# Experts' scatter in a mixture-of-experts kernel: the block outputs become the stationary operand, the residual reads the sums, the last round gathers nothing, and the output leaves in four parts

## What is computed

```
h2 = rms(x) * (1 + sc2) + sh2                       # 256 tokens x 1024
idx, w = the 8 best of 64 experts for each token    # weights sum to 2.5
moe  = (silu(h2 @ w_sh_gate) * (h2 @ w_sh_up)) @ w_sh_down                # shared expert
moe += sum over the token's experts e of
       w_e * ((silu(h2 @ w_gate_e) * (h2 @ w_up_e)) @ w_down_e)           # hidden width 256
out = x + gt2 * moe
```

## Time and profile before

| | |
|---|---|
| median of 3 runs | 1740.06 us (1738.6 to 1741.92) |
| profiled execution, its own time | 1738.21 us |
| its span, first to last instruction | 1736.6 us |
| mean granted clock | 0.986 |
| PE busy | 1661.4 us, 96% of the span |
| DVE, ACT busy | 971.8 us (56%), 688.5 us (40%) |
| pairs of blocks (count of L2944) | 34 |
| scatter matmuls, L1431 | 140 with `yhi`, 140 with `ylo`: 35 scatters of 8 |

### The profile page before, as it was taken

How to read it: one execution, slowest core, us unless ns; L and a number is a source line. 1 busy time by engine, 2 the same in 40 slices (tenths; PEclk the granted TensorE clock), 3 DMA queues, 4 the chain that set the end, 5 groups by cost and what they waited for, 6 DMA issues and landing times.

```text
span 1736.6 us, 26907 instructions
## 1 busy us (share of the span) xinstructions
PE 1661.4 (96%) x10642; PEld 1309.8 (75%) x10642; DVE 971.8 (56%) x1705; ACT 688.5 (40%) x1225; POOL 62.0 (4%) x48
## 2 busy tenths in 40 slices
PE   8889999998989999999999999999999999999997
PEld 6678999986789999878898989897544454545453
DVE  6967777769677777576756697665121212121212
ACT  2155434321554444465543577632222232323222
POOL 0100000001000000005110000000000000000000
PEclk9999999999999999999999999998999999999999
DMA  6222666752226667532402333336899999999993
GB/s 278 97 74 101 228 230 242 262 198 97 95 100 219 236 242 290 200 122 96 141 25 98 146 132 135 142 139 269 327 423 422 421 422 422 422 422 422 423 422 137
DMA packets 63963, 404.66 MB, mean 233 GB/s; under 512 B 12928, under 2 KB 14464, under 8 KB 15232
## 3 DMA queue, kind: packets, MB, share of 16 engines
q1 hardware_dynamic: 63440, 401.86, 59.3%
q10 hardware_dynamic: 432, 1.51, 0.2%
HBM read 401.91 MB, written 1.44 MB: 232 GB/s over the span
## 4 chain that ended last, share of the span: by engine, by line
PE 76%; DVE 16%; ACT 5%; issue 1%; DMA 0%; SPq 0%; DVEq 0%; ACTq 0%
PE ps L1441 20%; PE ps L847 19%; PE ps L988 10%; DVE big L2234 5%; PE ps L1414 4%; PE ps L1431 4%; PE ps L672 2%; DVE inv L2487 2%; DVE wlo L2298 2%; ACT whi L1634 2%; PE ps L1321 1%; DVE wlo L2665 1%; PE ps L1353 1%; PE ps L1382 1%; ACT wb L1842 1%
## 5 line engine op out<-in xcount | busy, mean ns | idle before, releaser
L2298 DVE TENSOR_TENSOR wlo<-ring,whi 128x2048 fp32r<-128x2048 f32 x76 | 174.2, 2292 | 90.3 <-ACT whi L1634 90.0
L847 PE MATMUL ps<-hg_hi,whi 128*128 128x272 f32 (+1 forms) x672 | 191.3, 285 | 2.4 <-DVE big L2430 2.4
L847 PE MATMUL ps<-hg_hi,wlo 128*128 128x272 f32 (+1 forms) x672 | 191.4, 285 | 0.0
L847 PE MATMUL ps<-hn_lo,whi 128*128 128x272 f32 (+1 forms) x672 | 190.8, 284 | 0.0
L1441 PE MATMUL ps<-big 128*64 128x512 f32 x816 | 181.8, 594 | 0.7 <-ACT big L2122 0.7
L1441 PE MATMUL ps<-ring,big 128*64 128x512 f32 x816 | 181.7, 594 | 0.0
L1634 ACT ACTIVATE whi<-ring 128x2048 fp32r<-128x2048 f32 x76 | 144.9, 1907 | 70.4 <-PE ps L847 51.8
L2951 DVE TENSOR_TENSOR ylo<-ps,yhi 128x512 fp32r<-128x512 f32 x68 | 47.0, 692 | 172.2 <-ACT yhi L2145 137.3
L672 PE MATMUL ps<-hn,ring 128*128 128x272 f32 x576 | 138.3, 398 | 0.0
L1441 PEld LDWEIGHTS ps<-big 128*64 128x64 f32 x816 | 57.5, 137 | 106.9 <-issue 106.6
L1441 PEld LDWEIGHTS ps<-ring,big 128*64 128x64 f32 x816 | 57.1, 137 | 107.2 <-issue 106.8
(11 more groups left out here) (456 smaller groups left out, 3585.9 us busy)
## 6 DMA issues: line engine op xcount, KB each, us to landing
ring<-in_stream SPq DMA_DIRECT2D x277, 1024.0 KB, 5.4
big<-in_stream SPq DMA_DIRECT2D x102, 1024.0 KB, 10.6
h<-in_xT SPq DMA_DIRECT2D x1, 1088.0 KB, 5.1
out_xT<-h SPq DMA_DIRECT2D x1, 1024.0 KB, 4.7
big<-in_consts ACTq DMA_DIRECT2D x1, 896.0 KB, 4.7
cst<-in_consts SPq DMA_DIRECT2D x1, 576.0 KB, 6.1
cs<-in_c_rows SPq DMA_DIRECT2D x1, 512.0 KB, 17.6
big<-in_consts ACTq DMA_DIRECT2D x1, 326.5 KB, 3.5
```

Source lines behind the costliest of these rows:

```text
L847: m = mm(out, a[:, at_:at_ + P], b[:, kept], start=first and i == 0, stop=last and i == 2)
L2298: v.tensor_tensor(wlo[j][:, :], ring[:, j, :], whi[d % 3][:, :], ALU.subtract).then_inc(wlo_ready, 1)
```

## The change

The scatter swaps its operands: 128 features of `yhi` or `ylo` are now stationary, and all 256 tokens of `STr` move. The sums then have features on the partitions, as `x` has them. `shared_down`, which starts these sums, is turned in the same way. The copies, the transposes back and their buffer and semaphores go, and DVE reads banks 4 to 7 itself. The fixed loop has 15 rounds (`FIXED`), the loop of `quads_n` follows, and the last round stands behind both as straight code without the next round's gather, its copies and its places. The last scatter is done in two halves, each after its own half of `ylo`. The output leaves in four transfers of two chunks each.

```diff
+FIXED = EXPERTS // 4 - 1
...
-            sp.wait_ge(x_ready, 24)
-            sp.dma_start(out, x).then_inc(out_done, 16)
-            sp.wait_ge(out_done, 16)
+            for i in range(4):
+                sp.wait_ge(x_ready, 16 + 2 * i + 2)
+                sp.dma_start(out[:, 2 * i:2 * i + 2, :], x[:, 2 * i:2 * i + 2, :]).then_inc(out_done, 16)
+            sp.wait_ge(out_done, 64)
...
+            def sums_of(c):
+
+                return ps[:, 4 + c // 2, (c % 2) * T:(c % 2 + 1) * T]
+
             def shared_down(t):
-                for half in range(2):
+                for c in range(4 * t, 4 * t + 4):
                     for f_ in range(2):
-                        m = mm(ps[:, 4 + 2 * t + half, :], hid[:, f_, t * P:(t + 1) * P], w_sh[:, f_, half * 512:(half + 1) * 512],
-                               start=f_ == 0, stop=False, skip_group_check=True)
+                        m = mm(sums_of(c), w_sh[:, f_, c * P:(c + 1) * P], hid[:, f_, :], start=f_ + c % 2 == 0, stop=False,
+                               skip_group_check=True)
                 return m
...
             def scatter(q, quarters=range(4), last=False):
 
-                for t, half in (divmod(quarter, 2) for quarter in quarters):
-                    for i, piece in enumerate((yhi, ylo)):
-                        m = mm(ps[:, 4 + 2 * t + half, :], STr[:, q, t * P:(t + 1) * P],
-                               piece[:, half * 512:(half + 1) * 512], start=False, stop=last and i == 1,
-                               skip_group_check=True)
+                for quarter in quarters:
+                    for c in range(2 * quarter, 2 * quarter + 2):
+                        for i, piece in enumerate((yhi, ylo)):
+                            m = mm(sums_of(c), piece[:, c * P:(c + 1) * P], STr[:, q, :], start=False, stop=last and i == 1,
+                                   skip_group_check=True)
                     if last:
                         m.then_inc(acc_full, 1)
...
-            def pair_of_blocks(quad, q, turn2):
+            def pair_of_blocks(quad, q, turn2, last=False):
...
-                if q == 1:
+                if q == 1 and not last:
                     pe.wait_ge(place_ready, 2 * quad + 4)
                     gather(0)
...
-                else:
+                elif not last:
                     gather(1)
...
-                turn_places(1 - q)
+                if q == 0 or not last:
+                    turn_places(1 - q)
...
-            with pe.Fori(0, EXPERTS // 4) as t_:
+            with pe.Fori(0, FIXED) as t_:
                 for q in range(2):
                     pair_of_blocks(t_, q, t_)
...
-                    pair_of_blocks(EXPERTS // 4 + t_, q, EXPERTS // 4 + t_)
-            pe.wait_ge(ylo_ready, EXPERTS + 4 * quads_n + 2)
-            scatter(1, last=True)
-
-            pe.wait_ge(acc_out, 4)
-            for k in range(DC):
-                for t in range(2):
-                    m = nc.tensor.transpose(ps[:, k // 2, (k % 2) * T + t * P:(k % 2) * T + (t + 1) * P],
-                                            acc_sb[:, t, k * P:(k + 1) * P], ident)
-                if k % 2:
-                    m.then_inc(y_full, 1)
+                    pair_of_blocks(FIXED + t_, q, FIXED + t_)
+            for q in range(2):
+                pair_of_blocks(FIXED + quads_n, q, FIXED + quads_n, last=True)
+            for half in range(2):
+                pe.wait_ge(ylo_ready, 4 * FIXED + 4 * quads_n + 5 + half)
+                scatter(1, range(2 * half, 2 * half + 2), last=True)
...
-            def pair_on_act(quad, q):
+            def pair_on_act(quad, q, last=False):
...
-                if q == 1:
+                if q == 1 and not last:
                     tokens_out(quad + 1, 0)
...
-                if q == 1:
+                if q == 1 and not last:
                     for i in range(1, 4):
                         tokens_out(quad + 1, i)
-                places_out(p + 1, 1 - q)
+                if q == 0 or not last:
+                    places_out(p + 1, 1 - q)
...
-            for g in range(2):
-                act.wait_ge(acc_full, g + 1)
-                f(acc_sb[:, 0, g * 512:(g + 1) * 512], ps[:, 4 + g, :], ACT.Copy).then_inc(acc_out, 1)
+            for q in range(2):
+                pair_on_act(FIXED + quads_n, q, last=True)
...
-            def pair_on_dve(quad, q):
+            def pair_on_dve(quad, q, last=False):
...
-                if q == 0:
+                if q == 0 and not last:
                     dve.wait_ge(t_full, p + 2)
                     places(quad + 1)
...
-            for g in range(2, 4):
-                dve.wait_ge(acc_full, g + 1)
-                v.tensor_copy(acc_sb[:, 1, (g - 2) * 512:(g - 1) * 512], ps[:, 4 + g, :]).then_inc(acc_out, 1)
+            for q in range(2):
+                pair_on_dve(FIXED + quads_n, q, last=True)
             for c in range(DC):
                 if c % 2 == 0:
-                    dve.wait_ge(y_full, c // 2 + 1)
-                v.scalar_tensor_tensor(x[:, c, :], flat[:, c * T:(c + 1) * T], mod[:, 40 + c:41 + c], x[:, c, :],
+                    dve.wait_ge(acc_full, c // 2 + 1)
+                v.scalar_tensor_tensor(x[:, c, :], flat[:, 2048 + c * T:2048 + (c + 1) * T], mod[:, 40 + c:41 + c], x[:, c, :],
                                        ALU.mult, ALU.add).then_inc(x_ready, 1)
```

More of the change, by code:

```diff
@@ L309, in build @@
         hg = region(27776, DC, 2 * P)
-        acc_sb = region(15488, 2, D)
         flat = ps[:, :, :].rearrange("p a b -> p (a b)")
@@ L469, in build @@
         acc_full = sem("acc_full")
-        acc_out = sem("acc_out")
-        y_full = sem("y_full")
         block = ctx.enter_context(nc.Block())
@@ L2151, in _ @@
             places_out(0, 0)
-            with act.Fori(0, EXPERTS // 4) as t:
+            with act.Fori(0, FIXED) as t:
                 for q in range(2):
@@ L2158, in _ @@
                 for q in range(2):
-                    pair_on_act(EXPERTS // 4 + t, q)
-            for g in range(2):
-                act.wait_ge(acc_full, g + 1)
-                f(acc_sb[:, 0, g * 512:(g + 1) * 512], ps[:, 4 + g, :], ACT.Copy).then_inc(acc_out, 1)
+                    pair_on_act(FIXED + t, q)
+            for q in range(2):
+                pair_on_act(FIXED + quads_n, q, last=True)
         @block.vector
@@ L2951, in pair_on_dve @@
                     v.tensor_tensor(ylo[:, o], ps[:, 3 - half, :], yhi[:, o], ALU.subtract).then_inc(ylo_ready, 1)
-            with dve.Fori(0, EXPERTS // 4) as t:
+            with dve.Fori(0, FIXED) as t:
                 for q in range(2):
@@ L2959, in _ @@
                 for q in range(2):
-                    pair_on_dve(EXPERTS // 4 + t, q)
-            for g in range(2, 4):
-                dve.wait_ge(acc_full, g + 1)
-                v.tensor_copy(acc_sb[:, 1, (g - 2) * 512:(g - 1) * 512], ps[:, 4 + g, :]).then_inc(acc_out, 1)
+                    pair_on_dve(FIXED + t, q)
+            for q in range(2):
+                pair_on_dve(FIXED + quads_n, q, last=True)
             for c in range(DC):
                 if c % 2 == 0:
-                    dve.wait_ge(y_full, c // 2 + 1)
-                v.scalar_tensor_tensor(x[:, c, :], flat[:, c * T:(c + 1) * T], mod[:, 40 + c:41 + c], x[:, c, :],
+                    dve.wait_ge(acc_full, c // 2 + 1)
+                v.scalar_tensor_tensor(x[:, c, :], flat[:, 2048 + c * T:2048 + (c + 1) * T], mod[:, 40 + c:41 + c], x[:, c, :],
                                        ALU.mult, ALU.add).then_inc(x_ready, 1)
```

## The result

| | before | after |
|---|---|---|
| median of 5 runs each | 1739.28 us (1738.55 to 1741.92) | 1730.51 us (1729.94 to 1732.69) |
| profiled execution, its span | 1736.6 us | 1730.9 us |
| first round's gate product to the end of the span | 515.75 us | 507.49 us |

The ratio is 0.9950, 95% interval 0.9936 to 0.9965: 8.8 us faster by the medians, with 9.0 forecast (1731.1 us, range 1728 to 1736). That the medians came within 0.2 us of the forecast is partly luck: further down, two medians of the same code lie 1.6 us apart, and the stretches add up to less than 9.0.

What follows compares the result with a forecast made beforehand. PE was taken to set the pace in the rounds, with transfers close behind, and a path through other engines after the last down product. Terms -3.36, -3.75, -2.2 and +0.3 sum to -9.0 us: 1740.06 to 1731.1, range 1728 to 1736.

Steps and rivals of the forecast that it cites:

- The rounds: Scatter in each pair, 16 matmuls of 256 columns for 8 of 512: +0.3 us for 34 pairs, bounds -0.7 and +1.0.
- Weight loads: Scatter: doubled loads cost nothing, hidden under earlier matmuls; rival: each 0.19 us load sets the pace, about 1770 us, chance 0.06.
- The last round: Last pair without gathers and places: down product starts at 1715.88 instead of 1719.24, -3.36 us, PE waiting for ACT's copy.
- The tail: Down product to first addition: 5.05 us instead of 8.80, -3.75 us, first half's scatter hidden, no copies or transposes in line.
- The output: Four transfers instead of one: last part lands about 2.5 us after issue instead of 4.7, -2.2 us, bounds -2.7 and -1.6.
- The sum: Whole kernel: -3.36 - 3.75 - 2.2 + 0.3 = -9.0 us, giving 1731.1 us.
- Late code: Rival, straight last round: code fetches no longer covered bring 2 to 5 us back, 1733 to 1736 us, chance 0.12.
- series: Rival, output: each part starts only when the one before has landed, -4.0 us in all, 1736.1 us, chance 0.06.

## Why the prediction was right

**The rounds.** This term was mis-sized: +0.3 was forecast, and it measured +0.99. I put the new scatter with `q == 1` at the first gather's 0.115 us, and it ran at 0.119 (1.90 us for 16). With `q == 0` my 0.118 held (2.09 us a pair before and after). The bound of +1.0 that I had worked out from 0.118 everywhere was the value. Why the gather is faster than the scatter at the same shape stays open; the order of accumulation is ruled out.

**Weight loads.** That they cost nothing was right for this change, but my reason was too strong. That a load "lies under the matmuls before it" holds only down to 0.110 us a matmul. The row of 0.19 is a duration, not a pace. The Trainium skill, page "TensorE: Matmul & The Clock Gate", section "LDWEIGHTS (loading the stationary operand)", gives 1 ns per 1.2 stationary columns. My estimate from that is 107 ns for 128 and 53 for 64; the runs agree as to the pace (0.110 and 0.060), while the record of one load shows 0.19. The rule in the same page's section "Part 3: Packing small matmuls — row/col tiling", that loads overlap only across groups of rows, is not borne out here: full loads of 128x128 lay under matmuls at 0.119.

**The last round.** Forecast -3.36, measured -3.21. The wait for the copy came as foreseen, 0.10 us longer: the down product started 0.94 after the transposes instead of 0.84. The copy itself was right (its end 0.80 after the transposes' start, 0.79 forecast); PE's start behind it took 0.14 instead of 0.05. The rest, 0.05, is the scatter's pace.

**The tail.** Forecast -3.75, measured -3.87. The two halves of the scatter ran where I had placed them, and DVE never stopped.

**The output.** Forecast -2.2, measured -2.16, but this closeness is luck in part. Between the end of the last issue and the end of the span lie 4.63 us before (1731.97 to 1736.6) and 2.76 after (1728.14 to 1730.9), a gain of 1.87 where I had 2.2. The other 0.3 comes from the issue itself, 0.67 us for 1 MB and 0.37 to 0.41 for a part, which my sum left out. And the 0.2 us outside the span, of which no term of mine speaks, is lost by splitting. The parts landed after 2.2 to 2.7 us, none growing to the 5 and more that parts in series would show.

**The sum.** The stretches give -8.26, or about -8.1 with what lies outside the span, against -9.0. Most of the difference is the scatter's pace.

**Rivals.** Late code is refuted for the stretch by the round with its gathers as straight code (one execution), series by the landings, weight loads at this width by the rounds of 29.58 us. The kernel stays bound by PE in the rounds, and in the last pair the weights were not waited for: the only wait ahead of its down product was for ACT's copy.

## To carry to other kernels

Behind the last matmul of this kernel nothing overlapped by itself: count the steps between the last product and the last byte, and let each step's orientation be that of the next, so that copies and turns fall away. Before a scatter is turned, compare the moving columns with the weight load's pace, not its duration: here 256 columns were just enough, and 128 cost 56 us. When work that nobody needs is cut, look for what it covered, and whether other work can be moved there.

## What the runs showed that I had not expected

- With 128 fp32r columns stationary, 256 moving columns start every 0.119 us and 128 every 0.110; with 64 stationary, 128 start every 0.060.
- SP issues a waited transfer every 0.52 us in a row of eight (4.16 us), though one issue is shown with about 0.4. In that run SP's delay behind DVE (1.44 us instead of 0.41) outweighed what the smaller last part saved (0.7 us).
- Splitting the output costs about 0.2 us outside the profile's span (1.77 to 1.90 us in nearly all executions, against 1.57 to 1.67 with one transfer). A comparison of spans alone doesn't see it.
- The 1220 us ahead of the rounds differ by 3.8 us between executions of nearly the same code, together with the mean granted clock. That is about as much as the largest single part of this change (3.87 us). What else goes with that clock is open.
